# Low parts of the delta net's and the stick's weights: the split moved from GpSimd to VectorE, with decays, SiLU, pair steps and head norms in other places

## What is computed

```
hn = rmsnorm(h); proj = hn @ w_in                       # 11 slices of w_in
q, k = l2norm(silu(conv4(dq))), l2norm(silu(conv4(dk)));  v = silu(conv4(dv))
g = -exp(a_log) * softplus(da + dt_bias); beta = sigmoid(db)
o_dn = rmsnorm(gated_delta_rule(q, k, v, g, beta)) * silu(dz)        # 8 heads, 128 / 256 wide
o_sb = stick_breaking_attention(rmsnorm(sq), rmsnorm(sk), sv)        # 8 heads, 128 wide
h = h + (sigmoid(gate_dn) * (o_dn @ w_branch_dn) + sigmoid(gate_sb) * (o_sb @ w_branch_sb)) @ w_out
h = h + swiglu(rmsnorm(h))
```

## Time and profile before

| | |
|---|---|
| median of 3 runs | 2865.19 us (2865.05 to 2865.75) |
| the profiled execution | 2861.57 us, of which the span of instructions is 2859.3 us |
| granted TensorE clock, mean | 0.993 |
| busy: PE, DVE, ACT, POOL | 2790.1, 1489.2, 1139.2, 513.2 us |
| delta net and stick | 1338 to 2442 us |

### The profile page before, as it was taken

The page is one execution under the profiler, slowest core; times in us unless marked ns, Lnnn a source line. Parts: engine busy times, 40 slices in busy tenths (PEclk is TensorE's granted clock), DMA queues, the critical chain, the costliest instruction groups (busy, mean ns, idle before and its releaser), DMA issues.

```text
span 2859.3 us, 37052 instructions
## 1 busy us (share of the span) xinstructions
PE 2790.1 (98%) x14453; PEld 2233.2 (78%) x14453; DVE 1489.2 (52%) x2096; ACT 1139.2 (40%) x1697; POOL 513.2 (18%) x297
## 2 busy tenths in 40 slices
PE   8999999999999999999999999999999999999999
PEld 4888888866656688887898888887868877788887
DVE  6734534257546633335754656554267775653443
ACT  4221212224444432223655555554466663432221
POOL 0000000023111100002444444434422223100000
PEclk9999999999999999999999999999999999999999
DMA  6422313143102322222211211111211112232222
GB/s 234 151 78 83 120 63 111 53 139 120 37 30 88 127 93 92 96 92 100 80 53 45 67 56 64 53 53 38 74 60 60 60 60 93 95 103 93 91 97 81
DMA packets 69871, 241.77 MB, mean 85 GB/s; under 512 B 8218, under 2 KB 8346, under 8 KB 69314
## 3 DMA queue, kind: packets, MB, share of 16 engines
q1 hardware_dynamic: 62032, 221.28, 22.9%
q10 hardware_dynamic: 7666, 18.13, 1.9%
HBM read 232.74 MB, written 6.64 MB: 84 GB/s over the span
## 4 chain that ended last, share of the span: by engine, by line
PE 87%; DVE 5%; ACT 5%; DMA 1%; issue 1%; ACTq 0%; DVEq 0%; POOL 0%; SPq 0%; POOLq 0%
PE ps L1098 61%; PE ps L1484 3%; PE ps L1288 2%; PE ps L1381 2%; PE ps L1257 2%; PE ps L1585 2%; PE ps L1421 1%; PE ps L1275 1%; PE ps L1128 1%; PE ps L1309 1%; PE ps L1413 1%; ACT r L461 1%; DVE UT L468 1%; PE ps L1266 1%; ACT w_hi L461 1%
## 5 line engine op out<-in xcount | busy, mean ns | idle before, releaser
L1098 PE MATMUL ps<-Nh,w_hi 128*128 128x512 f32 (+1 forms) x1808 | 660.5, 365 | 9.5 <-DVE Nl L468 4.9
L1098 PE MATMUL ps<-Nl,w_hi 128*128 128x512 f32 (+1 forms) x1808 | 630.0, 348 | 0.0
L1098 PE MATMUL ps<-Nh,w_lo 128*128 128x512 f32 (+1 forms) x1808 | 628.0, 347 | 0.0
L461 ACT ACTIVATE w_hi<-w_raw 128x1024 fp32r<-128x1024 f32 (+1 forms) x352 | 368.7, 1047 | 637.4 <-PE ps L1098 521.8
L468 POOL TENSOR_TENSOR w_lo<-w_raw,w_hi 128x1024 fp32r<-128x1024 f32 x125 | 308.0, 2464 | 750.4 <-ACT w_hi L461 746.7
L468 DVE TENSOR_TENSOR w_lo<-w_raw,w_hi 128x1024 fp32r<-128x1024 f32 (+1 forms) x227 | 281.8, 1242 | 257.5 <-ACT w_hi L461 247.8
L1098 PEld LDWEIGHTS ps<-Nh,w_hi 128*128 128x128 f32 x1808 | 342.6, 190 | 80.2 <-issue 30.1
L1098 PEld LDWEIGHTS ps<-Nl,w_hi 128*128 128x128 f32 x1808 | 342.7, 190 | 50.6 <-issue 5.8
L1098 PEld LDWEIGHTS ps<-Nh,w_lo 128*128 128x128 f32 x1808 | 342.4, 189 | 44.1
L1098 PE MATMUL ps<-x1h,w_hi 128*128 128x512 f32 (+1 forms) x784 | 272.3, 347 | 1.9 <-DVE x1l L479 1.9
L1098 PE MATMUL ps<-x1l,w_hi 128*128 128x512 f32 (+1 forms) x784 | 266.6, 340 | 0.0
(11 more groups left out here) (353 smaller groups left out, 4725.0 us busy)
## 6 DMA issues: line engine op xcount, KB each, us to landing
w_raw<-in_w_in SPq DMA_DIRECT2D x132, 512.0 KB, 3.5
w_raw<-in_w_proj SPq DMA_DIRECT2D x89, 512.0 KB, 3.4
w_raw<-in_w_ada SPq DMA_DIRECT2D x52, 512.0 KB, 4.1
w_raw<-in_w_out SPq DMA_DIRECT2D x48, 448.0 KB, 3.2
w_raw<-in_w_out SPq DMA_DIRECT2D x24, 512.0 KB, 3.4
w_raw<-in_w_mix_in SPq DMA_DIRECT2D x19, 512.0 KB, 3.5
w_raw<-in_w_bdn SPq DMA_DIRECT2D x16, 512.0 KB, 3.4
w_raw<-in_w_mix_out SPq DMA_DIRECT2D x8, 512.0 KB, 3.5
```

Source lines behind the costliest of these rows:

```text
L461: self.then_inc(self.e.activation(out, in_, func, **kw), sem)
L1098: ins = e.matmul(out[:, 512 * j:512 * j + n], a[:, kk, :], x[:, kk, c0:c0 + n], start=k == 0 and p == 0, stop=k == nt - 1 and p == 2)
```

## The change

The low parts of all units of w_proj from 3 on, and of the branch weights w_bdn and w_bsb, are now split on VectorE. `_POOLED` keeps only its first range. For the delta net and the stick the split stands in VectorE's list six product steps (`since == 6`) behind the last product of each unit, or at the end of the next unit if that comes first. In addition

- the high parts and splits of w_proj up to unit 3 come before the root of the norm at the beginning of the second block,
- the first round and the last but two of the delta net have their own times for bcast and decay (FIRST_ROUND, LAST_ROUND), the silu v of round 0 moves into round 1, and LATE_SCAN gives v0, siluv and s0 new times,
- `pairs` makes LT and both UTs for the two sizes first and both ATs after, with the semaphore counts that go with it,
- `head_norm` of the stick has ScalarE square its exponential, and VectorE makes three operations per column block instead of five or six, with gains prepared in gain_sb,
- the gates at the end of the stick are taken in smaller groups, and splits go with units from 81 on.

```diff
+FIRST_ROUND = ((58, "bcast"), (65, "decay"))
+LAST_ROUND = ((58, "bcast"), (64.5, "decay"))
...
-            (30.4, "stq2"), (37, "l2k"), (40, "lnk"), (45.3, "stk0"), (45.9, "stk1"), (45.9, "stk2"),
-            (59.1, "siluv"))
+            (30.4, "stq2"), (37, "l2k"), (40, "lnk"), (45.3, "stk0"), (45.9, "stk1"), (45.9, "stk2"))
...
-LATE_SCAN = ((7.95, "v0"), (7.95, "siluv"), (7.95, "s0"), (7.95, "k1"), (9.83, "v1"), (12.1, "s1"),
+LATE_SCAN = ((0.52, "v0"), (7.3, "siluv"), (5.2, "s0"), (7.95, "k1"), (9.83, "v1"), (12.1, "s1"),
...
-            steps += [(at, s, i + 2) for at, s in DECAYS]
+            steps += [(at, s, i + 2) for at, s in (FIRST_ROUND if i == 0 else LAST_ROUND if i + 3 == NH else DECAYS)]
+            steps += [(5.2, "siluv", 0)] if i == 1 else []
...
-_POOLED = [(split_of("w_mix_in", 4), split_of("w_mix_out", 0)),
-           (split_of("w_proj", 3), split_of("w_o2", 0))]
+_POOLED = [(split_of("w_mix_in", 4), split_of("w_mix_out", 0))]
...
     def pairs(h):
...
-            w.tt(lt, lt, b, ALU.mult, s.p_u)
+            w.tt(lt, lt, product(i, 0, n, C), ALU.mult, s.p_u)
             w.tt(u, lt, each(cs("level", n, n, 0), n, C), ALU.mult, s.p_u)
             w.tt(u, each(cs("ident", n, n), n, C), u, ALU.subtract, s.p_u)
+        for i, (c0, n, C) in enumerate(WIDE):
+            at, dt = (a[0:n, c0:c0 + C, 0:n] for a in (t.AT[h % 2], t.DT))
             w.wait_ge(s.p_pair, 4 * h + 2 * i + 2)
-            w.tt(at, b2, dt, ALU.mult, s.p_u)
+            w.tt(at, product(i, 1, n, C), dt, ALU.mult, s.p_u)
...
     def head_norm(h, i, ev):
...
+        w.wait_ge(s.k_exp, 2 * h + i + 1)
         for j, (c0, n) in enumerate(COLS2 if i else COLSM):
-            w.ts(v[:, c0:c0 + n], ps[:, B.of[(*ev, j)][0], 0:n], 1.0 / P, EPS, ALU.mult, ALU.add, s.k_v)
-        w.stt(tt, y, -0.5, v[:, cc], ALU.mult, ALU.mult, s.step)
-        w.tt(tt, tt, y, ALU.mult, s.step)
-        w.stt(y, tt, 1.5, y, ALU.add, ALU.mult, s.step)
+            w.stt(tt[:, c0:c0 + n], ps[:, B.of[(*ev, j)][0], 0:n], P * EPS, square[:, c0:c0 + n], ALU.add, ALU.mult, s.k_v)
+        w.stt(y, tt[:, cc], -384.0, y, ALU.add, ALU.mult, s.step)
...
+        if ended is not None and ev[0] in ("mm", "branch"):
+            since += 1
+            if since == 6:
+                lows(split_of(*ended), last)
+                ended = None
+        if ev[0] == "mm" and ev[3] == KT - 1 or ev[0] == "branch" and ev[2] % 4 == 3:
+            if ended is not None:
+                lows(split_of(*ended), last)
+            ended = ev[1:3] if ev[0] == "mm" else ("w_bdn", 2 * ev[1] + ev[2] // 4)
+            since = 0
...
-                for u in {77: (73, 74, 75), 78: (76, 77, 78)}.get(gating, (gating,)):
+                for u in {77: (73, 74), 78: (75,), 79: (76, 77), 80: (78, 79), 81: (80, 81)}.get(gating, (gating,)):
```

More of the change, by code:

```diff
@@ L553, in __init__ @@
         self.branch = new("branch")
-        self.k_raw, self.k_sq, self.k_mm, self.k_ln, self.k_v, self.k_exp, self.k_norm = (
-            new("k_raw"), new("k_sq"), new("k_mm"), new("k_ln"), new("k_v"), new("k_exp"), new("k_norm"))
+        self.k_raw, self.k_sq, self.k_mm, self.k_v, self.k_exp, self.k_norm = (
+            new("k_raw"), new("k_sq"), new("k_mm"), new("k_v"), new("k_exp"), new("k_norm"))
         self.z_mm, self.z_abs, self.z_ln, self.z_sp, self.vt_mm, self.vt = (
@@ L599, in __init__ @@
         self.eps_sq = mem.put("eps_sq", [P, 1])
+        self.gain_sb = mem.put("gain_sb", [P, 2])
         low = mem.at
@@ L965, in delta @@
         elif name == "pair":
-            for i, v in enumerate((1, 4, 8)):
+            for i, v in enumerate((1, 7, 8)):
                 chain.use((name, h, i), s.p_u, 8 * h + v)
@@ L1913, in scalar @@
     e.dma_start(h_spill, XV).then_inc(s.h_out, 16)
+    highs(split_of("w_proj", 0) - 1, last)
     root_ln(5, D, f[1], COLSX, None, t.eps_sq[:])
     root_exp(f[3], f[1])
-    highs(split_of("w_proj", 0) - 1, last)
     z4 = [tv[0], tv[2], f[0], f[1]]
@@ L2140, in head_norm @@
     def head_norm(h, i, ev):
-        w.wait_ge(s.k_norm, 3 * h + 2 * i)
+        w.wait_ge(s.k_norm, 2 * h + i)
         for j, (c0, n) in enumerate(COLS2 if i else COLSM):
             w.wait_ge(s.k_mm, 3 * h + i + j + 1)
-            w.act(t.sr[0][:, c0:c0 + n], ps[:, B.of[(*ev, j)][0], 0:n], ACT.Ln, s.k_ln, scale=1.0 / P,
+            w.act(t.sr[0][:, c0:c0 + n], ps[:, B.of[(*ev, j)][0], 0:n], ACT.Ln, s.act_step, scale=1.0 / P,
                   bias=cs("eps", n=1))
         cc = slice(0, T2) if i else MS
-        w.act(t.sr[1][:, cc], t.sr[0][:, cc], ACT.Exp, s.k_exp, scale=-0.5)
+        w.act(t.sr[1][:, cc], t.sr[0][:, cc], ACT.Exp, s.act_step, scale=-0.5)
+        w.act(t.sr[0][:, cc], t.sr[1][:, cc], ACT.Square, s.k_exp)
     def scores(h, jb):
@@ L2644, in vector @@
     ffn(1, XV, t.h2h[:, :, 0:TX], t.h2l[:, :, 0:TX], f[0:2], f[2:4], COLSX, GX, t.GM[:, 1], last)
+    lows(split_of("w_proj", 0) - 1, last)
     root_v(5, D, f[0], COLSX, None, EPS * EPS)
     root(5, f[0], f[2], f[3])
-    lows(split_of("w_proj", 0) - 1, last)
     w.wait_ge(*summed(6, s, 6))
@@ L2695, in pairs, with product @@
     def pairs(h):
+        def product(i, j, n, C):
+            bank = ps[:, B.of["pair", h, j][0], :] if i == 0 else ps[:, B.of["pair", h, 2][0], j * n:]
+            return in_chunks(bank, n, C)
         for i, (c0, n, C) in enumerate(WIDE):
-            b, b2 = (in_chunks(ps[:, B.of["pair", h, j][0], :] if i == 0 else ps[:, B.of["pair", h, 2][0], j * n:], n, C)
-                     for j in range(2))
-            dt, at, lt = (a[0:n, c0:c0 + C, 0:n] for a in (t.DT, t.AT[h % 2], t.LT))
+            lt = t.LT[0:n, c0:c0 + C, 0:n]
             u = t.UT[h % 2][0:n, 0, c0:c0 + C, 0:n]
@@ L2793, in vector @@
     tapping, tapped, adding = None, -1, None
+    lows(split_of("w_proj", 0), last)
     w.wait_ge(s.mod_hi, 5 * KT)
+    ended, since = None, 0
     for ev in DELTA:
@@ L2844, in vector @@
     branch(*adding)
+    lows(split_of(*ended), last)
     w.wait_ge(s.n_hi, 2 * NH)
     w.wait_ge(s.n_lo, 2 * NH)
+    for i, (name, factor) in enumerate((("sbq", -1.0 / 256 * float(P) ** -0.5), ("sbk", -1.0 / 256))):
+        w.ts(t.gain_sb[:, i:i + 1], sm(name), factor, None, ALU.mult, None, s.step)
     def head_norm(h, i, ev):
         cc = slice(0, T2) if i else MS
-        v, tt, y = t.sr[5], t.sr[0][:, cc], t.sr[1][:, cc]
+        tt, square, y = t.sr[5], t.sr[0], t.sr[1][:, cc]
+        w.wait_ge(s.k_exp, 2 * h + i + 1)
         for j, (c0, n) in enumerate(COLS2 if i else COLSM):
-            w.wait_ge(s.k_ln, 3 * h + i + j + 1)
-            w.ts(v[:, c0:c0 + n], ps[:, B.of[(*ev, j)][0], 0:n], 1.0 / P, EPS, ALU.mult, ALU.add, s.k_v)
-        w.wait_ge(s.k_exp, 2 * h + i + 1)
-        w.stt(tt, y, -0.5, v[:, cc], ALU.mult, ALU.mult, s.step)
-        w.tt(tt, tt, y, ALU.mult, s.step)
-        w.stt(y, tt, 1.5, y, ALU.add, ALU.mult, s.step)
+            w.stt(tt[:, c0:c0 + n], ps[:, B.of[(*ev, j)][0], 0:n], P * EPS, square[:, c0:c0 + n], ALU.add, ALU.mult, s.k_v)
+        w.stt(y, tt[:, cc], -384.0, y, ALU.add, ALU.mult, s.step)
         dst = t.Fs[h % 2][:, i, cc]
-        w.stt(dst, dst, sm("sbq" if i == 0 else "sbk"), y, ALU.mult, ALU.mult, s.k_norm)
-        if i == 0:
-            w.ts(dst, dst, float(P) ** -0.5, None, ALU.mult, None, s.k_norm)
+        w.stt(dst, dst, t.gain_sb[:, i:i + 1], y, ALU.mult, ALU.mult, s.k_norm)
     def softplus(h, jb):
@@ L2924, in vector @@
             adding = None
+        if ended is not None and ev[0] in ("mm", "branch"):
+            since += 1
+            if since == 6:
+                lows(split_of(*ended), last)
+                ended = None
+        if ev[0] == "mm" and ev[3] == KT - 1 and ev[2] < 81 or ev[0] == "branch" and ev[2] == KT - 1 and ev[1] < NH - 1:
+            if ended is not None:
+                lows(split_of(*ended), last)
+            ended = ev[1:3] if ev[0] == "mm" else ("w_bsb", ev[1])
+            since = 0
         if ev[0] in ("mm", "branch"):
             if gating is not None and ev[0] == "mm" and ev[3] == 1:
-                for u in {77: (73, 74, 75), 78: (76, 77, 78)}.get(gating, (gating,)):
+                for u in {77: (73, 74), 78: (75,), 79: (76, 77), 80: (78, 79), 81: (80, 81)}.get(gating, (gating,)):
                     gate(u)
-                if gating > 83:
+                if gating > 80 and gating != 82:
                     lows(split_of("w_proj", gating), split_of("w_o2", KT - 1))
```

6 lines of the change are left out of this document (3 added, 3 removed).

## The result

The changed kernel takes 2889.82 us (2885.11 to 2890.70, 4 runs), before 2865.47 us beside it: the ratio is 1.0083, 95% interval 1.0071 to 1.0095. That is 24 us slower, outside the range of 2850 to 2871, on the side of rival C, and further than C went.

A forecast was written before the change was run, and what follows sets the result against it. TensorE, busy for 98% of the span, was taken as the bound, so only its waits or low clock count. Terms sum to -4.1, plus 1.4 for locks: -2.7, a median of 2862.5 us, counted as the same; range 2850 to 2871.

The forecast's parts named there:

- rival C: Branch products' adds into acc and accs: splits ahead of them make TensorE wait, 8 x 1.2 = +9.8; 2872 to 2877; chance 0.20.
- Lists: Delta net's first and last rounds: decays moved earlier block VectorE at the DT product, +2.2 and +0.4.
- mechanism of the first round: VectorE waits 3.5 at DT ahead of the gains; pair(2) waits 5.1 to 7.1 in place of 4.44; +2.2.
- The last round: 1922 to 1952: VectorE blocks at DT, TensorE waits about 3 for a free bank; +0.4 (-1.5 to +2.5).
- Regular turns: Second turns of the regular rounds: with both UTs made before AT, four waits of 1.19 go, -4.8.
- Locks: GpSimd's LM and ol meet VectorE's splits once per round: 8 x 0.17 = +1.4 (0 to 9.6).
- Start: Step into the delta net (1338): unit 3's split ahead of root_v, +0.4 (0 to +1.2) on the wait for Nl.
- first turn: At 1397: a split and an LM delay the UT product, +2.0 (0 to +3) on a wait of some 2.4.
- first head: 1369 to 1383: gbt's wait of 1.2 goes and about half of r's 3.1; -2.7 (-3.4 to -1.2).
- The adds of acc and accs: Stick: the delta net's last add behind a split, +0.6; in the tail one add behind a split, +0.9.
- The head norm's gain at SP: Stick's start: with two products fewer ahead of sbf, the wait for SP (4.2) gets 0.9 shorter.
- The other signs: Second turns wait for nothing; TensorE waits about 5 at pair(2) for qk; SP's wait some 3.3; vv's taps near 0.77.

The follow-up runs named there:

- shift32: The kernel before with one unused tile of 2 floats ahead of the activations, every tile behind it 32 bytes further on: 2874.29 us, ratio 1.0034.
- norm_128: The kernel before with the new head norm alone, gain_sb given 128 bytes so that no tile moves modulo 128: 2867.08 us, ratio 0.9999.
- last_only: The kernel before with only the last round's lists changed (bcast, decay of head 7 earlier; v0, silu v, s0 at new times): 2866.90 us, ratio 1.0006.
- splits_only: The kernel before with the splits moved to VectorE, early root order and new gates; old lists, pairs, head norm and memory map: 2871.17 us, ratio 1.0028.
- splits_lm: As splits_only, with GpSimd's LM waiting for both UT steps instead of for LT: 2865.09 us, ratio 0.9997 against the kernel before.
- after_128_lists: The changed kernel with gain_sb given 128 bytes and the delta net's lists of before: 2874.92 us, ratio 1.0031 against the kernel before.

## Why the prediction was wrong, point by point

**The step that failed** is the one that opens it: "Only a wait of TensorE, or a low clock of it, can be won or lost", with the diff said to touch the two stages and the step into them alone. TensorE's pace changed at full clock, in stages that the diff leaves alone. The new tile gain_sb moves every activation by 32 bytes; shift32 measures that at 10.3 us, and norm_128 shows no further cost of the norm that can be told. I costed the head norm by its operations and passed over the line that allocates 8 bytes.

That alone would not have saved the forecast: with the 10 taken off, the changed kernel is still some 14 above before, where 2.7 below was forecast. The terms that follow make up that part.

**Lists, +2.6 forecast, 6.5 measured.** The mechanism of the first round was right: VectorE waits 3.32 at DT and does the gains behind it.

```profile
1525.80 0.96 DVE L469 TENSOR_TENSOR DT<-DT,const 128x512 f32<-128x512 f32 x2 [3.32 <-ACT DT L462]
1526.80 2.45 DVE L480 SCALAR_TENSOR_TENSOR O<-O,small,r 128x512 f32<-128x512 f32 x2
```

The size was off: I had one wait, at the pairs. There are two, for zz (ScalarE copies the next zz only when VectorE is through with the last, and waits 3.85 for that) and then for qk:

```profile
1531.59 0.36 PE L1100 MATMUL ps<-Nh,w_hi 128*128 128x264 f32 x1 [4.25 <-ACT zz L462]
...
1538.03 4.00 PE L1361 MATMUL ps<-qk 128*128 128x128 f32 x20 [3.46 <-DVE qk L480]
```

7.7 us in place of 4.44, not 5.1 to 7.1. That "the pairs wait for them" was right, but zz waits for the gains before that. The last round came as described: 3.1 for acc in last_only, "about 3" forecast.

**Regular turns, -4.8 forecast, about 0 measured in the changed kernel.** That the turn needs nothing but UT was wrong. The waits for AT from 1540 to 1900 are 4.7 before and 5.0 after. In the changed kernel LM's lock (the UT step of 1.68) and then AT stand before the turn, and the wait is 1.25:

```profile
1633.45 0.63 PE L1370 MATMUL ps<-const,UT 128*128 128x128 f32 x4 [1.25 <-DVE AT L469]
```

The row of before that named AT as what ended the wait said so; I took the name for an accident of VectorE's order, and it was the bank.

**Locks, +1.4 forecast.** They cost some 7 (splits_only against splits_lm, 3.8 of it seen as idle time of TensorE). I had the rule and put my choice at its low end, because TensorE had slack at x and u; the waited chain was LT, UT, UT, one product of which stood behind LM in each head.

**Start, first turn, tail.** The wait for Nl grew 0.9 (forecast +0.4, 0 to 1.2). The first turn came near, 4.3 against 4.4. The first head did not: gbt's wait of 1.2 went, but r's grew from 3.1 to 3.6, -0.7 for the -2.7 forecast. The adds of acc and accs were costed at 0.6 and 0.9 and wait 10.7 in all, from 2.6 in the earlier trace rows. Rival C had this place right, and its sign (5 or more) came; its price for it was near too, 9.8 (the product written there, 8 x 1.2, is 9.6) against 8.1, and what it lacked were the tiles, the lists and the order of pairs. The head norm's gain at SP was 0.5, not 0.9. The other signs: vv's taps came to 0.77 in the median as forecast, pair(2) waited 3.5 for qk, and the second turns moved their wait to the first ones.

**Sum.** Map 10, lists 6.5, splits 7 (all of it undone by LM's later start), norm 0: 23.5 of 24. That this comes out so close is luck. The order of pairs isn't in it, which costs 8.6 by itself and 2.5 between splits_only and after_128_lists (with the norm); taking map and lists back together gave 12 to 15, not 16.5; and each of these figures has an interval of some 3 us to either side. The parts overlap.

Not settled: the low clock that the changed kernel's profile shows near 1596, with TensorE busy all through and no wait over 0.2 us close ahead of it.

```profile
1592.00:1596.00 4.00, 4.00 (x27) 3.89 (x26) 3.24 (x5) 2.57 (x5) 0.00 (x0) 0.75 0.32 116
1596.00:1600.00 4.00, 4.00 (x13) 3.37 (x13) 1.97 (x4) 0.00 (x0) 0.00 (x0) 0.50 0.06 22
```

The second run of the same kernel has 1.00 there, and splits_only has 0.50 at 1833, where before has 1.00. It comes and goes from run to run, as part of the spread of every kernel's times, and what sets it was not tried. Waits below 0.3 us were not followed up. What share of the 10 us is each tile's was not tried either, nor how much of the price of an order lies in the low clock that comes with it.

## What to carry to other kernels

Before costing an edit by its instructions, look at every line that allocates: a tile placed in front of others moves all of them, and an unused one of 8 bytes cost 10 us of 2865, more than any single part of this change. Compare two traces at a mark ahead of the edit: a difference there can't come from the edited instructions. When a wait names a producer, ask which resource of it is waited for, its result or the bank that it reads: only a change of the bank tells them apart. When work leaves an engine, ask what starts earlier on it, and whom that now meets.

## What the runs showed of the hardware

The pace of TensorE's long products depends on where the tiles of activations start in SBUF, at the same granted clock. With x1, h1, N, h2 and h3 at multiples of 128 bytes, TensorE has 2430 products in 430 us of the first FFN; 32 bytes behind, 2402, and the whole kernel takes 10.3 us more; 64 behind, 2414 and 3.8 us; 128 behind, 2439. All activations moved together, so which operand sets the pace isn't shown, and since a move by 128 changes it too, the start modulo 128 is not the whole of it. And with the splits gone from GpSimd, VectorE's second UT step took 1658 ns in the mean of 8 heads, against 928 with GpSimd's LM behind it, where six heads have 0.69 and two, in which GpSimd's ol overlaps, still 1.64:

```profile
L467 DVE TENSOR_TENSOR UT<-const,UT 128x512 f32<-128x512 f32 x8 | 13.3, 1658 | 0.3
```

```profile
L467 DVE TENSOR_TENSOR UT<-const,UT 128x512 f32<-128x512 f32 x8 | 7.4, 928 | 0.3
```

The first row is of splits_only, the second of splits_lm.
